# Order of copies, rotations and weight splits in the second block's mixer and feed-forward of a two-block transformer kernel

## The reference, cut to what matters

```python
def hybrid_mixer_2(h, cos, sin, w_in, ...):
    proj = h @ w_in                                    # 256 x 2844
    (fq, fk, fv, ff, nq, kc, vc, ks, vs, kw, vw, ng, dq, dk, dv) = jnp.split(proj, splits, axis=-1)
    o_fox = fox_attention(heads(fq, 4), heads(fk, 4), heads(fv, 4), log_f)
    gates = jax.nn.sigmoid(ng + b_nsa_gate).reshape(B, S, NSA_HEADS, 3)
    o_nsa = nsa_attention(rope(nq, 8), rope(kc, 2), heads(vc, 2), rope(ks, 2), heads(vs, 2),
                          rope(kw, 2), heads(vw, 2), gates, ...)   # compressed, selected, window
    o_dil = dilated_attention(rope(dq, 4), rope(dk, 4), heads(dv, 4))
    return jnp.concatenate([o_fox, o_nsa, o_dil], axis=-1) @ w_out

def conv_ffn(h, w_up, conv_w, conv_b, w_down):
    c = conv_b + three causal taps of (h @ w_up)
    a, b = jnp.split(c, 2, axis=-1)
    return (jax.nn.silu(a) * b) @ w_down

for l in range(2):
    x = x + rms_norm_2(hybrid_mixer_2(rms_norm_2(x, ...), ...), ...)
    x = x + rms_norm_2(conv_ffn(rms_norm_2(x, ...), ...), ...)
```

## Time and profile before

| | us |
|---|---|
| timed runs (3), lowest, median, highest | 2152.99, 2163.15, 2165.8 |
| profiled execution | 2151.45 |
| its span, first to last instruction | 2149.7 |
| PE, DVE, ACT busy over the span | 2024.2, 1407.6, 1158.9 |
| first mixer of block 2 (about) | 1323 to 1524 |
| second mixer of block 2 (about) | 1742 to 1939 |

### The profile page before, as it was taken

The page is one execution under the profiler, slowest core; times in us unless marked ns, Lnnn a source line. Parts: engine busy times, 40 slices in busy tenths (PEclk is TensorE's granted clock), DMA queues, the critical chain, the costliest instruction groups (busy, mean ns, idle before and its releaser), DMA issues.

```text
span 2149.7 us, 39543 instructions
## 1 busy us (share of the span) xinstructions
PE 2024.2 (94%) x15240; PEld 1919.3 (89%) x15240; DVE 1407.6 (65%) x2072; ACT 1158.9 (54%) x1847; POOL 132.7 (6%) x153
## 2 busy tenths in 40 slices
PE   7999989989999999989989999898999989898998
PEld 7999979989999999979989999676899977678998
DVE  5765887566656655887556656763698476638973
ACT  5444665554445444765554445654576447546653
POOL 1061000010000001000010001000200000002000
PEclk9999999999999999999989999888999999898999
DMA  5555334445455546334445454430254543304643
GB/s 217 200 167 197 137 123 135 153 174 195 166 178 200 181 161 210 125 122 140 155 166 189 164 177 163 138 118 20 99 196 165 201 140 130 106 1 139 213 159 115
DMA packets 53533, 329.80 MB, mean 153 GB/s; under 512 B 5936, under 2 KB 6704, under 8 KB 27952
## 3 DMA queue, kind: packets, MB, share of 16 engines
q1 hardware_dynamic: 53424, 328.34, 44.3%
HBM read 327.27 MB, written 1.05 MB: 153 GB/s over the span
## 4 chain that ended last, share of the span: by engine, by line
PE 73%; DVE 10%; ACT 6%; DVEq 4%; DMA 3%; issue 3%; POOL 0%; POOLq 0%; ACTq 0%; SPq 0%
PE bank L653 19%; PE bank L654 19%; PE bank L655 19%; DVE w_lo L632 4%; DMA raw<-in_w 3%; PE bank L700 3%; ACT w_hi L593 2%; DVE conv L1358 1%; PE bank L665 1%; PE bank L1647 1%; PE bank L667 1%; DVEq L1023 1%; PE bank L674 1%; PE bank L1631 1%; PE bank L1648 1%
## 5 line engine op out<-in xcount | busy, mean ns | idle before, releaser
L632 DVE TENSOR_TENSOR w_lo<-raw,w_hi 128x2048 fp32r<-128x2048 f32 (+3 forms) x348 | 673.9, 1940 | 354.4 <-ACT w_hi L593 326.8
L653 PE MATMUL bank<-h_hi,w_hi 128*128 128x256 f32 x2704 | 784.1, 290 | 11.3 <-DVE w_lo L632 10.1
L654 PE MATMUL bank<-h_lo,w_hi 128*128 128x256 f32 x2704 | 772.3, 286 | 0.0
L655 PE MATMUL bank<-h_hi,w_lo 128*128 128x256 f32 x2704 | 772.0, 286 | 0.0
L593 ACT ACTIVATE w_hi<-raw 128x2048 fp32r<-128x2048 f32 (+2 forms) x346 | 560.4, 1622 | 160.4 <-DMA raw<-in_w 108.7
L653 PEld LDWEIGHTS bank<-h_hi,w_hi 128*128 128x128 f32 x2704 | 527.0, 195 | 17.1 <-DVE w_lo L632 13.4
L654 PEld LDWEIGHTS bank<-h_lo,w_hi 128*128 128x128 f32 x2704 | 527.0, 195 | 1.3
L655 PEld LDWEIGHTS bank<-h_hi,w_lo 128*128 128x128 f32 x2704 | 526.2, 195 | 0.0
L653 PE MATMUL bank<-hid_hi,w_hi 128*128 128x256 f32 x1056 | 295.4, 280 | 0.0
L654 PE MATMUL bank<-hid_lo,w_hi 128*128 128x256 f32 x1056 | 295.4, 280 | 0.0
L655 PE MATMUL bank<-hid_hi,w_lo 128*128 128x256 f32 x1056 | 295.4, 280 | 0.0
(11 more groups left out here) (339 smaller groups left out, 3006.3 us busy)
## 6 DMA issues: line engine op xcount, KB each, us to landing
raw<-in_w SPq DMA_DIRECT2D x198, 1024.0 KB, 4.8
raw<-in_w SPq DMA_DIRECT2D x96, 704.0 KB, 4.1
raw<-in_w SPq DMA_DIRECT2D x52, 768.0 KB, 4.2
raw<-in_w SPq DMA_DIRECT2D x8, 512.0 KB, 3.5
raw<-in_w SPq DMA_DIRECT2D x4, 576.0 KB, 3.7
x<-in_x SPq DMA_DIRECT2D x1, 1024.0 KB, 4.9
out<-x SPq DMA_DIRECT2D x4, 256.0 KB, 2.4
const<-in_const SPq DMA_DIRECT2D x1, 548.0 KB, 5.8
```

Source lines behind the costliest of these rows:

```text
L632: dve.tensor_tensor(w_lo[:, s % SPLIT_SLOTS, 0:n], raw[:, s % RAW_SLOTS, 0:n], w_hi[:, s % SPLIT_SLOTS, 0:n].bitcast(F32), ALU.subtract).t ...
L653: pe.matmul(out, hi, x_hi, start=start, stop=False, skip_group_check=skip)
L654: pe.matmul(out, hi, x_lo, start=False, stop=False, skip_group_check=skip)
L655: return pe.matmul(out, lo, x_hi, start=False, stop=stop, skip_group_check=skip)
```

## The change

Four things are reordered; PE, POOL and SP keep their order, and no instruction is added or removed.

1. `EVAC2` is ACT's own list: `STEPS2` with each pair S(n), T(n - 3) exchanged for n from 3. ACT copies the transposes of head n - 3 ahead of the splits, the exponentials and the norms of step S(n).
2. In the opening, ACT's split of unit ("va", 0) (unit 7 of the layer) moves behind the gates' sigmoid. DVE's low part of it moves behind the third rotation, and its low part of ("va", 1) (unit 8) behind the maxima of S(0).
3. In the second block's feed-forward, ACT splits unit 5 ahead of the first gated unit, and the low parts of units 5, 6 and 7 come one gated unit earlier on both engines; gated unit 3 has none.
4. At the end of each of the first block's four feed-forwards DVE adds residual 6 ahead of the low part of the next stage's first unit.

```diff
+EVAC2 = list(STEPS2)
+for n in range(3, len(HEADS2)):
+    at = EVAC2.index(("S", n))
+    EVAC2[at], EVAC2[at + 1] = EVAC2[at + 1], EVAC2[at]
@@ ffn_dve
             split.next = base + 12
+            residual(6, 0)
             split.until(base + 12)
-            residual(6, 0)
             raw_low(dve, n1, l2, n2_, 6, gain1(l2, n2_, 6))
@@ mixer2_act
-            for kind, i in STEPS2:
+            for kind, i in EVAC2:
...
-                if g in UNIT_OF2 and kind != "O":
+                if g in UNIT_OF2 and kind != "O" and g != ("vb", 1):
                     split.until(at2 + UNIT_OF2[g] + AHEAD)
...
                         act.activation(gates2[:], gates2[:], ACT.Sigmoid).then_inc(gates_ready.sem, 1)
+                        split.until(at2 + UNIT_OF2[g] + AHEAD)
@@ mixer2_dve
-                if g in UNIT_OF2 and kind != "O":
+                if g in UNIT_OF2 and kind != "O" and g not in (("vb", 1), ("f", 0)):
                     split.until(at2 + UNIT_OF2[g] + AHEAD)
...
                     dve.tensor_tensor(part, part, rot, ALU.add).then_inc(rotated.sem, 1)
+                    if i == 3:
+                        split.until(at2 + UNIT_OF2["vb", 1] + AHEAD)
...
                     softmax_dve_max(dve, work, l, g, ATTN_SCALE, bias, probs2, row2, i % PROBS2, max2_ready)
+                    if i == 0:
+                        split.until(at2 + UNIT_OF2["f", 0] + AHEAD)
@@ ffn2_act
+            split.until(at + FFN_AHEAD + 1)
             for j in range(4):
-                gated(j, 0, lambda: split.until(at + j + FFN_AHEAD))
+                gated(j, 0, lambda: split.until(at + min(j + 1, 3) + FFN_AHEAD))
```

## The result

The changed kernel took 2107.4 us (median of 4 runs, 2103.8 to 2109.5) against 2158.4 for the kernel before (4 runs): ratio 0.9765, 95% interval 0.9741 to 0.979. Run again among the experiments it took 2104.9 (6 runs), ratio 0.9749, 0.972 to 0.9779. The forecast was 2126, range 2106 to 2150: the direction held, and so did the range, but only just: the first median lies 1.4 us inside its edge and the second 1.1 outside. The saving was 51 us where I had 37. The number comes out at rival 2's 2105.

A forecast was written before the change was run, and what follows sets the result against it. Latency between engines in block 2's two attention mixers was taken to bound the kernel, no engine being full there. (6.5 + 4 + 7 + 1) x 2 = 37 us off the median of 2163.15 gave 2126 us, range 2106 to 2150.

The forecast's parts named there:

- rival 2: Block 2's mixers: with most gaps gone the clock stays up; saving 58 us, 2105 us; chance 0.15.
- Part A: Mixer opening, both layers: rotations ahead of splits remove the waits at S(0) and R(0); 6.5 us per layer, 4.3 to 6.7.
- Part B: Mixer up to f(6): copies of transposes ahead of exponentials remove three waits, a new one comes at ct(0); 4 us per layer.
- with a tail of 1.4: Mixer, at ct(0): the new wait of 1.8 to 5.8 us per layer brings a slow-clock tail of 1.4 us.
- Part C: Rest of the mixer: waits at T(9), J(0), J(1) and T(20) go or shrink; 7 us per layer, 5 to 9.
- about 0.7 of tails: Rest of the mixer: slow-clock tails add about 0.7 us to the 6.3 us of waits, making 7 per layer.
- Part D: Feed-forward opening, both layers: unit 5's wait of 3.67 us gives way to 0.9 and 2.1 at units 6 and 7; gain 1.
- Part E: Residual 6 ahead of a split, four times: under PE's last 66 products, so nothing, within +-2 us for all four.
- Rival 1: Mixers: the pace moves to DVE, ACT and loads, Part B and most of Part C return as waits; 2145 us; chance 0.15.
- Rival 3: Mixers: copies ahead of about nine ACT weight splits per layer delay each by 1.7 us; slower, 2181 us; chance 0.08.
- B is nearer 7: Mixer: if no wait appears at L1587, Part B saves nearer 7 us per layer.
- the other signs of error: Mixers: any wait on w_lo over 1 us, or waits at L1625 still over 8 us per layer.

The follow-up runs named there:

- the gelu experiment: Changed kernel with two of ACT's weight splits moved behind the second gelu: 2104.6 us, ratio 0.9747 to the kernel before.
- the two edits that gave nothing alone: Each on the changed kernel: copies of a tile's last values ahead of the exponentials, 2106.4 us; two ACT weight splits behind the second gelu, 2104.6 us.
- both edits: Changed kernel with two ACT splits behind the second gelu and copies of a tile's last values ahead of the exponentials: 2093.1 us, ratio 0.9703.
- the fastest kernel: Kernel with both edits, with DVE's low part at S(14) moved behind the sums of head 15: 2089.6 us, ratio 0.9669 to the kernel before.

## Why the prediction was right or wrong

**What bounds the kernel** held: latency between engines in the two mixers. The experiments that removed such waits together gained, and neither DVE nor ACT was full.

**Part A**, 6.5 per layer: right for this change (10 to 13 us for both layers by the runs, 6.9 and 6.8 by the traces), but not by its own steps alone. They count A as if nothing stood behind it. Alone it gives 7 for both layers together.

**Part B**, 4 per layer: the wait at ct(0) fell inside the predicted 1.8 to 5.8 (4.5), and B is 2.7 and 1.4 in the change, 5.1 and 3.3 with the copies alone. The step that failed is "with a tail of 1.4": the gelu experiment puts it at 3.4 to 3.9. From S(1) to S(11) the granted clock is 0.93 before and 0.93 now, so the one fall behind ct(0) costs as much clock as the three tails that went.

**Part C**, 7 per layer, from 5 to 9: 10 in the traces. The waits came where they were predicted, except that head 12's products met theirs before J(0) did. Their sum was put too high: idle time fell by 4.2 and 3.2 us, where I had 6.3 (a wait of 4.2 in place of 5.2 is 1.0 and not the 2.3 that I added up). What outweighs it is "about 0.7 of tails": the better clock gave 5.9 and 6.7. The copies as a whole, B and C, made 30 us (25 to 35) where I had 22.

**Part D**, 1 per layer: 2.6 and 3.5 in every trace that has it; 1.6 alone by the runs (not certain), about 4 with the copies, D and E together. The waits at units 6 and 7 came shorter than forecast (0.5 for 0.9 and 1.7 for 2.1), and "likely with a tail" was wrong: there was none.

**Part E**, 0 within +-2: -0.6 in the first trace of the changed kernel, +0.6 in its second. It wasn't run alone, and its size stays open.

**The sum** fell short in the size of the tails. "Such a tail of 11 to 17 products costs 0.09 us each, 1.0 to 1.5 us" was read off one unit in the earlier trace rows. But the small matmuls of attention behind a wait run slow as well, and the fall lasts through them: 3.1 to 4.7 us for one wait in the compression stretch, and 3.2 from S(11) to S(13) of the kernel before, behind this wait:

```profile
1431.54 0.55 PE L1625 MATMUL bank<-const,probs 128*128 128x128 f32 x3 [0.66 <-ACT scr L1735]
```

With 22 us of clock instead of 11 the sum of 37 is 48, against 42 between the traces; so some 5 us of it are waits that I took to be worth more than they were, mostly in C.

**"The saving is the same in each, so I take it from the median"** failed too. The profiled pair is 42 us apart and the medians 51: 2151.45 and 2109.53 lie 7 below the one median and 2 above the other. The 53 timed runs of the kernel before among the experiments show what differs: their granted clocks go from 0.970 for the fastest (2145.5) to 0.958 for the slowest (2170.9), with a median of 0.962. The profiled run had 0.967. It was one of the good ones, and by (1 - 0.962) x 2156 = 82 against 71 the typical run loses 11 us more to the clock. The changed kernel's ten runs scatter by 8 us instead of 25, around a median clock of 0.978. So the change gives some 35 us of clock in a typical run, and 22 in the pair. The base moved as well: with 2158.4 for the 2163.15 of three runs, the forecast of 37 would have read 2121.

**Rival 2** named the mechanism that was missing, more clock than my tails count, and its 2105 is the time. Of the 37 us of lost speed that it took from the earlier trace rows, 18 are gone in the changed kernel's first trace and 22 in its second; it had 24 and my tails 11. It expected 1.8 us at ct(0), where 4.5 stood, so it is right by its clock term and not in full, and part of the agreement in the number is luck. Its "a stretch of small attention matmuls stays thin without any wait" is refuted: with both edits, from S(0) to the wait at J(0), PE has no wait above 1.4 us and this clock:

```profile
1344.00:1437.00 93.00, 89.19 (x572) 71.74 (x573) 74.60 (x147) 69.03 (x150) 0.00 (x0) 1.00 0.42 148
```

**Rival 1** did not happen in the change as a whole, but it is what happens to single edits: the opening without copies, and the two edits that gave nothing alone. **Rival 3** is refuted. **"B is nearer 7"** and the other signs of error did not appear.

The Trainium skill (TensorE: Matmul & The Clock Gate, "What's actually happening") says that the point at which the clock changes varies from run to run, by half a microsecond at a kernel's first transition, because the window in which the gate looks at PE does not start with the kernel. The traces agree that it varies, and here it is worth more: the changed kernel's two profiles, with the same program, are 0.9 to 1.2 us apart in the first layer up to S(17) and 4.2 from S(18) on. Over the same work, from S(17) to S(18), the granted clock is 0.56 in the first and 0.94 in the second:

```profile
1451.10:1459.70 8.60, 8.60 (x37) 6.72 (x36) 2.53 (x6) 2.79 (x8) 0.00 (x0) 0.56 0.01 2
1450.10:1455.50 5.40, 5.40 (x36) 4.47 (x35) 2.54 (x6) 2.81 (x8) 0.00 (x0) 0.94 0.02 3
```

That the gate's window is the cause is the skill's word; no run here shows it.

## What to carry to other kernels

Price a wait of the tensor engine by what runs behind it: here waits of 2.35 and 1.87 us cost 7 and 5 in front of small matmuls, and 1.7 us cost only itself in front of a dense stretch, nearly every time. When the clock is part of the price, look at the granted clock of several timed runs before taking a saving from one profile: the profiled run may be a lucky one. When an edit removes the wait it was made for and gives no time, don't drop it: look up which wait took its place, remove that one too, and time the two together. A piece moved out of one chain must leave the whole chain free: between maxima and sums it cost what it had saved, behind the sums it paid.

## What was not expected of the hardware

The price of the clock does not follow the length of one idle stretch alone. The 1.71 us in the feed-forward's opening stand at 22 places of eleven traces, two in each, and left the clock up at 21 of them; in the fastest kernel's first layer it fell. Among the small matmuls of the mixer, 1.88 us in the earlier trace rows, 2.35 us in the compression stretch and 0.66 us at T(9) of the kernel before were each followed by the low clock within about a microsecond, and 1.86 us at J(0) within two. Yet the 1.3 us at head step 10 with both edits were not. And the clock can fall for longer or shorter at the same place of the same program, which by itself moves later work by 3 us in one trace; between two kernels with the same code in that stretch it was 6. What decides it was not tried.
